# Two stacked model blocks: a reordered projection and delta rule, and compression weights loaded ahead

## The chip, the cores and the metric

One core of a Trainium2 chip runs the whole program. The metric is the device time of one execution, in microseconds (us). The kernel before takes 2895.86 us, the median of three runs (2894.96 to 2896.51).

## The reference

256 tokens of width 1024 in fp32 pass through a first block of two layers and a second block of four. What matters here:

```
first block, for l in 0, 1:
  mod = silu(c) @ ada_w[l] + ada_b[l]          # 1024 x 9216: shifts, scales and gates of the layer
  x += 0.5 (1 + g1) * swiglu(modulate(x))      # width 2816
  h = modulate(x);  qkv, z, b, a, q_lat, kv_lat, k_pe, gates = split(h @ w_in)
  q, k, v = silu(causal_conv4(qkv));  q, k to unit length
  o_a = gated_delta_rule(q, k, v, g, beta)     # 8 heads of 128, chunks of 64 tokens
     per chunk: t_inv = (I + m)^-1,  m strictly lower triangular 64 x 64
  o_b = latent attention;  x += (1 + g2) * (mixed branches @ w_out);  second swiglu
second block, layers 0 and 3 (NSA): block compression of keys and values
     gelu(windows @ w1) @ w2 with w1 of 2048 x 256, then compressed, chosen and window attention
```

## The kernel before

One program per engine is written out by hand, and each engine runs its instructions in that order. All weights come as **units** of at most 1 MB, numbered in one list (`unit`, `cols`, `plan_ffn`, `plan_ada`, lines 195 to 290). SyncE loads unit u into one of four raw buffers once unit u-4 is through with it (`sync_program`, line 2878). For most units ScalarE then writes the rounded high part to one of three `wsp` buffers and VectorE the rest (line 348 `ready_act`, line 363 `ready_dve`); TensorE multiplies both parts. `reach` (line 307) says how far ahead of unit u these splits may be issued: three splits past u. Units of ada_w are not split: VectorE adds them up in eight steps (`ada_step`, line 388), TensorE sums the partitions (`ada_pe`) and VectorE adds the bias (`mod_dve`). Units of how "raw" (the NSA compression weights) are multiplied from the raw buffer itself.

**Projection and convolution** (`conv_pe` line 1239, `conv_act` 1274, `conv_dve` 1317). w_in's first 3072 columns are twelve units of 256 columns, qkv 0 to 11; the unit of 16 columns for b and a ("ba") stands third in the list. Units 0 and 1 are multiplied before the norm's root is known (`lins_early`, 490: chunks of unit 0, the sum of squares, chunks of unit 1, the spread of the root, the rest). Then come ba, whose chunks wait for the normalized input pair by pair, and unit 2. After each unit i from 2 to 9 TensorE sums the squares of unit i-2 in head channels, once ScalarE has them (semaphore `SQQ`):

```
                if 2 <= i < 10:
                    e.wait_ge(*SQQ.at((l, i - 2)))
                    sums(e, bank["qksum", l], 4 * (i - 2), SQ2[i % 2], 2).then_inc(*CSUM.up((l, i - 2)))
```

The squares of unit 0 come by this chain: VectorE scales the product (`scaled`), ScalarE adds the shift and makes the last tap's product, VectorE adds three taps for each of two tiles (`taps_dve`, 1340), ScalarE takes silu and the square (`conv_silu_act`, 1307). `gates_act` and `gates_dve` (1355, 1372) make beta and the decay from ba.

**Delta rule** (`delta_pe` 1477, `delta_act` 1650, `delta_dve` 1686, `delta_pool` 1763). There are four chunks c; a tile has the 64 tokens of a chunk for head 2hp on partitions 0 to 63 and for head 2hp+1 on 64 to 127 (q = 0, 1), four head pairs side by side. GpSimd and VectorE make m and the decayed qk. The inverse T is built in six levels s = 0 to 5 by doubling blocks. At each level, chunk by chunk: 8 products x = m T (64x64 each), VectorE masks x into XX, 8 products add T x to T in PSUM and (s < 5) 8 add its transpose, ScalarE copies T and its transpose (512 columns together) back to UT. Operand and result of a product use the same half of the partitions, so the two heads of a pair use two of the array's four 64x64 tiles. Level 0 starts from an identity that eight matmuls of 512 columns write. Between the levels stand the transposes of k and v (`turned`) and two ada_w parts. The tail (`un`, `w`, `ws`, `kv`, `outs`) runs the recurrence; two more ada_w parts stand in it. `take` and `give` (406, 423) pass the eight PSUM banks on, first given first taken.

**NSA** (`nsa_pe` 2454, `nsa_act` 2550, `nsa_dve` 2597). TensorE multiplies kvc 0 and 1, gate, q 0, the first half of the compression weights (two raw units), q 1, the second half (two raw units), q 2, a transpose after GELU, q 3 and so on.

Of the kernel before, what the change touches and what calls it, by code (L numbers as in the profile page):

```python
# [17 lines left out]
NR = 4  # L18
# [12 lines left out]
NCONST = C_FREQ + 8  # L31
# [78 lines left out]
def build(nc, A, cst, out):  # L110
    ctx = ExitStack()
    with ctx:  # L112
# [51 lines left out]
        out_in = count("out_written")  # L164
        RAW = [count(f"raw{i}_landed") for i in range(NR)]
# [70 lines left out]

        w256 = [256]
        plan_ada(8)
        for l in range(2):
            plan_ffn(2 * l, A["ffn1_w1"][l], A["ffn1_w3"][l], A["ffn1_w2"][l], True)  # L240
            wi = A["w_in"][l]
            cols(("qkv", l), wi, w256 * 2, 0)
            cols(("ba", l), wi, [16], 4096)
            cols(("qkv", l), wi, w256 * 10, 512)
            cols(("z", l), wi, w256 * 3, 3072)
            plan_ada(4, "steps")
# [10 lines left out]
            cols(("up", l), A["mla_w_q_up"][l], [384] * 4, 0, "rope")  # L257
            cols(("up", l), A["mla_w_kv_up"][l], [512] * 4, 0)
# [8 lines left out]
        for i in range(4):  # L267
            kind, j = i % 3, i // 3
            if kind == 0:
# [4 lines left out]
                for s in range(2):  # L274
                    for n in "kv":
                        unit(("cmp", j), A[f"nsa_cmp_{n}_w1_2"][j].rearrange("(k p) n -> p k n", p=128)[:, 8 * s:8 * s + 8, :], 8, 256, "raw")
                    cols(("q", j), wi, w256, 256 + 256 * s)
# [212 lines left out]
        def lins_early(e, us, ps, n):  # L490
# [748 lines left out]
        def conv_pe(e, l, n):  # L1239
            for i in range(12):  # L1240
                if i == 2:
                    take(e, ("qksum", l))
                    u = U["ba", l][0]
                    b = take(e, ("ba", l))
                    lin(e, u, b, hH, hL, h_pairs(n)).then_inc(*MM.up(u))
                    give(("ba", l), GAC.at((l, "rows")))
# [7 lines left out]
                lin(e, u, b, hH, hL).then_inc(*MM.up(u))  # L1254
                give(("qkv", l, i), CVA.at((l, i)))
                if i == 2:
# [6 lines left out]
                if i == 4:  # L1263
                    decays_pe(e, l)
# [9 lines left out]
        def conv_act(e, l):  # L1274
            for i in range(12):
                if i == 2:
                    gates_act(e, l)
                if i == 5:
# [38 lines left out]
        def conv_dve(e, l):  # L1317
# [4 lines left out]
            for i in range(12):  # L1322
                if i == 2:
                    gates_dve(e, l)
                if i == 5:
                    decays_dve(e, l)
                    sums_dve(e, l)
                if i:
# [7 lines left out]
                if i >= 10:  # L1336
                    for q in range(2):
                        unit_dve(e, l, 2 * i - 16 + q)
# [95 lines left out]
        XX = [ar(6144 + 256 * c, 4, 64) for c in range(4)]  # L1434
        UT = [ar(9216 + 512 * c, 2, 4, 64) for c in range(4)]
        KT, KD, VT = ([ar(o + 512 * c, 4, 128) for c in range(4)] for o in (11264, 7168, 15360))
# [22 lines left out]
        def level(s):  # L1459

            return C[:, C_LV + 64 * s:C_LV + 64 * s + 64].unsqueeze(1).broadcast_to([128, 4, 64])
# [5 lines left out]
        def delta_ada(l):  # L1467

            return [nada[U["z", l][2] + 1 + i] for i in range(4)]
# [7 lines left out]
        def delta_pe(e, l):  # L1477
# [17 lines left out]
            for t in range(2):  # L1495
# [7 lines left out]
            def turned(name, c):  # L1503
# [6 lines left out]
                give((l, name, c), DVC.at((l, "kd", c)) if name == "kt" else DAC.at((l, "v", c)))  # L1510

            for s in range(6):
                for c in range(4):
                    b = take(e, (l, "x", s, c))
                    if s:
                        e.wait_ge(*DAC.at((l, "ut", s - 1, c)))
                    else:
                        e.wait_ge(*DVC.at((l, "m", c)))
                    for hp, q in both():
                        u = UT[c][half(q), 0, hp, :] if s else ident[half(q), half(q)]  # L1520
                        ins = e.matmul(P[b][half(q), 64 * hp:64 * hp + 64], MKQ[c][half(q), 0, hp, :], u, start=True, stop=True)
                    ins.then_inc(*DMM.up((l, "x", s, c)))
                    give((l, "x", s, c), DVC.at((l, "x", s, c)))
                if s == 0:
                    for c in range(4):
                        b = take(e, (l, "ut", c))
                        for q in range(2):
                            i64 = ident[half(q), half(q)]
                            e.matmul(v3(P[b][half(q), :], 8), i64, i64.unsqueeze(1).broadcast_to([64, 8, 64]), start=True, stop=False)
                    e.wait_ge(*SIL.at((l, 11)))  # L1530
                if s < 4:
                    turned("kt", s)
                    turned("vt", s)
                if s in (3, 4):
                    ada_pe(e, delta_ada(l)[s - 3])
                for c in range(4):
                    b = bank[l, "ut", c]
                    e.wait_ge(*DVC.at((l, "x", s, c)))
                    for hp, q in both():
                        t = UT[c][half(q), 1, hp, :] if s else ident[half(q), half(q)]  # L1540
                        x = XX[c][half(q), hp, :]
                        ins = e.matmul(P[b][half(q), 64 * hp:64 * hp + 64], t, x, start=False, stop=s == 5)
                    if s < 5:
                        for hp, q in both():
                            t = UT[c][half(q), 1, hp, :] if s else ident[half(q), half(q)]
                            x = XX[c][half(q), hp, :]
                            ins = e.matmul(P[b][half(q), 256 + 64 * hp:320 + 64 * hp], x, t, start=False, stop=s == 4)
                    ins.then_inc(*DMM.up((l, "ut", s, c)))
                    if s == 5:
                        give((l, "ut", c), DAC.at((l, "ut", 5, c)))  # L1550

            def un(c):
                b = take(e, (l, "un", c))
                e.wait_ge(*DAC.at((l, "ut", 5, c)))
# [6 lines left out]
            def w(t):  # L1561
                bs = [take(e, (l, "w", t, q)) for q in range(2)]
                for r in range(2):
                    c = 2 * t + r
                    e.wait_ge(*DAC.at((l, "ut", 5, c)))
# [72 lines left out]
            ada_pe(e, delta_ada(l)[2])  # L1638
# [6 lines left out]
            ada_pe(e, delta_ada(l)[3])  # L1645
# [4 lines left out]
        def delta_act(e, l):  # L1650
# [3 lines left out]
            for c in range(4):  # L1654
                e.wait_ge(*DMM.at((l, "eb", c // 2)))
                e.activation(EB[c].rearrange("p h j -> p (h j)"), P[bank[l, "eb", c]][:, :], ACT.Exp).then_inc(*DAC.up((l, "eb", c)))
            for i in (10, 11):
                conv_silu_act(e, l, i)
            ready_act(e, U["qkv", l][11])
            for s in range(6):  # L1660
                n = 512 if s < 5 else 256
                if s < 4:
                    e.wait_ge(*DMM.at((l, "vt", s)))
                    for hp in range(4):
                        ins = e.activation(VT[s][:, hp, :], P[bank[l, "vt", s]][:, 128 * hp:128 * hp + 128], ACT.Copy, scale=pair_col(BB, s, hp))
                    ins.then_inc(*DAC.up((l, "v", s)))
                for c in range(4):
                    e.wait_ge(*DMM.at((l, "ut", s, c)))
# [1414 lines left out]
```

## Time and profile before

| | us |
|---|---|
| median of three runs | 2895.86 |
| the profiled execution | 2896.91 |
| its span | 2895.1 |
| TensorE matmuls busy | 2795.2 (97%) |
| VectorE busy | 2106.0 (73%) |
| ScalarE busy | 1474.1 (51%) |
| GpSimd busy | 153.7 (5%) |

Times in the rows are microseconds from the span's start. PE is TensorE's matmuls, PEld its weight loads, DVE VectorE, ACT ScalarE, POOL GpSimd, SP SyncE. In brackets stands how long the engine was idle before the first instruction of the row, and who ended it. A matmul of fp32 operands has two records in the trace, one of fp32r operands has one. L65 (matmul), L68 (transpose), L71 (activation), L74 (tensor_tensor), L82 (scalar_tensor_tensor) are helpers that all code calls.

### The profile page before, as it was taken

The page shows a single profiled execution, that of the slowest core. Times are in us where ns is not written, and L with a number is a line of the kernel's source. Part 1 is how long each engine was busy: PE and PEld are TensorE (multiplying, and loading weights), DVE is VectorE, ACT ScalarE, POOL GpSimd, SP SyncE. Part 2 cuts the span into 40 slices and gives each one's busy share as a digit, 9 for nine tenths or more (in the row PEclk, how much of TensorE's full clock was granted, in tenths as well). Part 3 has the DMA queues.
Part 4 walks back from the last instruction along what each step waited for, and adds up shares of the span by engine and source line. Part 5 has one row for each costly group of instructions (what it writes and reads, how often), then busy time and mean ns, then how long its engine had stood idle before and what let it go on. Part 6 is the DMA issues. An engine that isn't in the chain of part 4 may idle for free. (4 is left out here: it accounts for less than half of the span.)

```text
span 2895.1 us, 53856 instructions
## 1 busy us (share of the span) xinstructions
PE 2795.2 (97%) x22820; PEld 2500.7 (86%) x22820; DVE 2106.0 (73%) x3321; ACT 1474.1 (51%) x2010; POOL 153.7 (5%) x257
## 2 busy tenths in 40 slices
PE   7998999999999989999999999999999999999998
PEld 6888899888888888998988878889788988887887
DVE  7886867669888877676786587765776677667774
ACT  3546644555455466445554355544554355435552
POOL 1000000200000000002000040000100000005000
PEclk9999999999999999999999999999999999999999
DMA  9775336537767743374475624555365556561552
GB/s 304 252 247 162 105 117 214 180 131 257 247 216 259 258 146 118 103 224 156 150 250 182 207 90 132 186 178 175 117 204 181 184 174 196 170 220 59 170 186 96
DMA packets 516703, 521.42 MB, mean 180 GB/s; under 512 B 16503, under 2 KB 513728, under 8 KB 516464
## 3 DMA queue, kind: packets, MB, share of 16 engines
q1 hardware_dynamic: 513856, 517.28, 54.9%
q8 instruction: 180, 2.95, 0.4%
q0 software_dynamic: 816, 0.27, 0.1%
q10 hardware_dynamic: 1792, 0.44, 0.1%
q14 instruction: 59, 0.48, 0.1%
HBM read 516.90 MB, written 1.05 MB: 179 GB/s over the span
## 5 line engine op out<-in xcount | busy, mean ns | idle before, releaser
L65 PE MATMUL P<-HX,wsp 128*128 128x512 f32 (+1 forms) x9920 | 1536.5, 317 | 28.0 <-DVE wsp L74 21.8
L65 PEld LDWEIGHTS P<-HX,wsp 128*128 128x128 f32 x9920 | 1386.7, 190 | 157.9 <-issue 28.8
L74 DVE TENSOR_TENSOR wsp<-raw,wsp 128x2048 fp32r<-128x2048 f32 (+3 forms) x440 | 945.8, 2152 | 321.1 <-ACT wsp L71 320.3
L71 ACT ACTIVATE wsp<-raw 128x2048 fp32r<-128x2048 f32 (+3 forms) x440 | 790.7, 1799 | 521.0 <-PE P L65 445.2
L65 PE MATMUL P<-FG,wsp 128*128 128x256 f32 (+1 forms) x2816 | 496.5, 338 | 0.0
L65 PEld LDWEIGHTS P<-FG,wsp 128*128 128x128 f32 x2816 | 428.7, 188 | 62.8 <-DVE wsp L74 1.2
L71 ACT ACTIVATE arena<-P 128x512 f32<-128x512 f32 (+3 forms) x379 | 210.6, 564 | 484.6 <-PE P L65 470.1
L74 DVE TENSOR_TENSOR arena<-arena,P 128x512 f32<-128x512 f32 (+2 forms) x226 | 147.0, 652 | 164.6 <-ACT arena L71 134.9
L82 DVE SCALAR_TENSOR_TENSOR ACC<-raw,sm,ACC 128x256 f32<-128x256 f32 x476 | 230.9, 485 | 16.6
L65 PE MATMUL P<-arena 64*64 64x64 f32 (+9 forms) x4000 | 226.8, 260 | 14.9 <-ACT arena L71 9.6
L65 PEld LDWEIGHTS P<-arena 64*64 64x64 f32 (+3 forms) x4000 | 182.6, 146 | 55.6 <-issue 31.0
L65 PE MATMUL P<-GX,wsp 128*128 128x256 f32 (+1 forms) x1592 | 227.8, 303 | 0.8 <-DVE GX L74 0.8
L65 PEld LDWEIGHTS P<-GX,wsp 128*128 128x128 f32 x1592 | 210.3, 191 | 13.5 <-DVE GX L74 1.1
L79 POOL TENSOR_SCALAR arena<-arena,sm 128x128 f32<-128x128 f32 x192 | 104.9, 557 | 1268.5 <-DVE sm L97 1265.9
L71 ACT ACTIVATE arena<-arena,sm 128x128 f32<-128x128 f32 (+1 forms) x206 | 91.5, 449 | 56.1 <-DVE sm L88 51.8
L71 ACT ACTIVATE arena<-arena 128x512 f32<-128x512 f32 (+2 forms) x174 | 105.3, 613 | 20.3 <-DVE arena L74 17.3
L71 ACT ACTIVATE FG<-arena 128x512 fp32r<-128x512 f32 x88 | 55.6, 632 | 114.0 <-DVE arena L74 102.4
L74 DVE TENSOR_TENSOR arena<-arena 128x512 f32<-128x512 f32 x144 | 98.8, 690 | 7.7 <-ACT arena L71 3.3
L68 PE MATMUL P<-C,arena 128*128 128x128 f32 x410 | 67.8, 298 | 30.3 <-POOL arena L79 15.6
L71 ACT ACT_TABLE_LOAD x62 | 79.5, 1283 | 17.1 <-issue 10.3
L88 DVE CUSTOM_DVE_ANT_0 arena<-P,C 128x128 f32<-128x128 f32 x192 | 59.7, 351 | 35.7 <-PE P L65 35.3
L68 PEld LDWEIGHTS P<-C,arena 128*128 128x128 f32 x410 | 48.4, 150 | 42.9 <-DMA arena<-in_norm_ffn 11.0
(119 smaller groups left out, 1556.1 us busy)
## 6 DMA issues: line engine op xcount, KB each, us to landing
raw<-in_ffn_w SPq DMA_DIRECT2D x120, 1024.0 KB, 5.1
raw<-in_ada_w SPq DMA_DIRECT2D x72, 1024.0 KB, 5.0
raw<-in_w_in SPq DMA_DIRECT2D x52, 1024.0 KB, 5.0
raw<-in_ffn_w_gate SPq DMA_DIRECT2D x44, 1024.0 KB, 5.1
raw<-in_ffn_w_up SPq DMA_DIRECT2D x44, 1024.0 KB, 5.1
raw<-in_ffn_w_down SPq DMA_DIRECT2D x32, 1024.0 KB, 5.0
raw<-in_nsa_w_in SPq DMA_DIRECT2D x20, 1024.0 KB, 8.0
raw<-in_ffn_w SPq DMA_DIRECT2D x16, 768.0 KB, 4.4
```

The costliest lines, as they stand in the source:

```text
L65: return self if self.e is None else self.e.matmul(*a, skip_group_check=True, **k)
L68: return self if self.e is None else self.e.transpose(*a)
L71: return self if self.e is None else self.e.activation(*a, **k)
L74: return self if self.e is None else self.e.tensor_tensor(*a)
L79: return self.e.tensor_scalar(o, a, s1, None, op0) if op1 is None else self.e.tensor_scalar(o, a, s1, s2, op0, op1)
L82: return self if self.e is None else self.e.scalar_tensor_tensor(out=o, in0=a, scalar=s, in1=b, op0=op0, op1=op1)
L88: return self.e.tensor_tensor_reduce(o, a, b, scale, 3.0e38, ALU.add, ALU.min, least)
```

## The change

- The ba unit moves from behind qkv unit 1 to behind unit 2, in the list and on all engines; unit 2 now takes the input pair by pair. `decays` moves one unit later. In `conv_act` the splits of units 0 and 1 are issued ahead of the shift. `lins_early` does five more chunks' worth of matmuls (30 in place of 18) between the sum of squares and the spread. VectorE scales the last two k tiles ahead of the taps of unit 10.
- The delta rule works on two halves t of two chunks. Level 0 needs no product: VectorE makes (masked m) + I. Then five levels: 16 products per half whose result goes to the other half of the partitions, one mask of 512 columns, and an update in which T's and the transpose's products alternate over all four 64x64 tiles. T and its transpose lie in two banks and are copied one after the other.
- Two ada_w parts per layer leave the delta levels for the latent up-projections (behind up 1 and up 4).
- The first half of the NSA compression weights (2 MB per NSA layer) is loaded in a feed-forward before it (f = 3 and 6) into free room; GELU is issued ahead of ScalarE's next splits, and VectorE makes the keys ahead of one split.
- In the first feed-forward the ada_w parts stand one unit pair earlier.

```diff
-                if ada and i % 4 and i < 11:
+                if ada and (i % 4 and i < 11 if f else i % 4 != 3 and i < 10):
...
-            cols(("qkv", l), wi, w256 * 2, 0)
+            cols(("qkv", l), wi, w256 * 3, 0)
             cols(("ba", l), wi, [16], 4096)
-            cols(("qkv", l), wi, w256 * 10, 512)
+            cols(("qkv", l), wi, w256 * 9, 768)
             cols(("z", l), wi, w256 * 3, 3072)
-            plan_ada(4, "steps")
+            plan_ada(2, "steps")
...
+            for i in range(4):
+                cols(("up", l), A["mla_w_q_up"][l], [384], 384 * i, "rope")
+                if i == 1:
+                    plan_ada(1)
+            for i in range(4):
+                cols(("up", l), A["mla_w_kv_up"][l], [512], 512 * i)
+                if i == 0:
+                    plan_ada(1)
...
             chunks_of(0, range(5))
             sums_pe(e, n)
-            chunks_of(1, range(3))
+            chunks_of(1, range(4))
+            chunks_of(0, (5,))
             spread_pe(e, n)
-            chunks_of(0, (5,))
-            chunks_of(1, range(3, 6))
+            chunks_of(1, range(4, 6))
...
                 if i == 2:
                     take(e, ("qksum", l))
+                if i == 3:
                     u = U["ba", l][0]
                     b = take(e, ("ba", l))
-                    lin(e, u, b, hH, hL, h_pairs(n)).then_inc(*MM.up(u))
+                    lin(e, u, b, hH, hL).then_inc(*MM.up(u))
...
-                lin(e, u, b, hH, hL).then_inc(*MM.up(u))
+                lin(e, u, b, hH, hL, h_pairs(n) if i == 2 else None).then_inc(*MM.up(u))
...
                 if i < 2:
+                    ready_act(e, u)
                     e.wait_ge(*CVS.at((l, i, "scaled")))
...
+                if i == 11:
+                    for q in range(2):
+                        unit_dve(e, l, 6 + q)
                 if i:
                     taps_dve(e, l, i - 1)
...
+            def first(t):
+                u, v = take(e, (l, "u", t)), take(e, (l, "t", t))
+                e.wait_ge(*DVC.at((l, "t1", t)))
+                for x in range(8):
+                    for q in range(2):
+                        i64, w = ident[half(q), half(q)], T1ST[t][half(q), x, :]
+                        o = 256 * (x // 4) + 64 * (x % 4)
+                        e.matmul(P[u][half(q), o:o + 64], w, i64, start=x == 0, stop=False)
+                        ins = e.matmul(P[v][half(1 - q), o:o + 64], i64, w, start=x == 0, stop=False)
...
+            def update(s, t):
...
+                    for q in range(2):
+                        T, W = UT[c][half(1 - q), 1, hp, :], XX[t][half(1 - q), x, :]
+                        ins = e.matmul(P[u][half(q), o:o + 64], T, W, start=False, stop=s == 5)
+                        if s < 5:
+                            ins = e.matmul(P[v][half(1 - q), o:o + 64], W, T, start=False, stop=s == 4)
...
+            first(0)
+            first(1)
+            for s in range(1, 6):
+                products(s, 0)
+                products(s, 1)
+                if s < 3:
+                    eb(s - 1)
+                if s >= 2:
+                    turned("kt", s - 2)
...
+                if s >= 3:
+                    turned("vt", s - 3)
...
+                update(s, 0)
+                update(s, 1)
...
+                for j, f in ((0, 3), (1, 6)):
+                    if u in U["f3", f][4:6]:
+                        i = U["f3", f].index(u) - 4
+                        e.wait_ge(*MM.at(U["f3", f][0]))
+                        e.dma_start(W1[i], cmp_src(j, "kv"[i], 0)).then_inc(*w1_in[i].up(j, 16))
```

## Rows read from the trace of the kernel before

**Rows 1.** The page, part 1: busy time by engine.

```profile
PE 2795.2 (97%) x22820; PEld 2500.7 (86%) x22820; DVE 2106.0 (73%) x3321; ACT 1474.1 (51%) x2010; POOL 153.7 (5%) x257
```

**Rows 2.** Stretches, delta rule of layer 0: length, busy by engine, PEclk, DMA share, GB/s.

```profile
333.50:343.50 10.00, 7.67 (x105) 5.51 (x104) 9.75 (x19) 5.71 (x11) 5.99 (x8) 1.00 0.26 90
343.50:385.90 42.40, 41.23 (x1153) 37.69 (x1155) 29.22 (x62) 21.88 (x44) 0.00 (x0) 1.00 0.24 78
385.90:404.70 18.80, 18.41 (x534) 16.90 (x530) 14.68 (x46) 6.28 (x14) 0.00 (x0) 1.00 0.35 115
```

**Rows 3.** Groups by form, TensorE, 343.5 to 385.8.

```profile
L65 PE MATMUL P<-arena 64*64 64x64 f32 x894 | 27.6, 219 | 1.1 <-issue 1.1
L65 PE MATMUL P<-C,arena 64*64 64x64 f32 x128 | 4.6, 219 | 1.0 <-DVE arena L74 1.0
L68 PE MATMUL P<-C,arena 128*128 128x128 f32 x32 | 4.4, 280 | 0.0
L65 PE MATMUL P<-C 64*64 64x512 f32 x16 | 3.6, 589 | 0.0
L65 PE MATMUL P<-arena,C 64*64 64x64 f32 x64 | 2.6, 220 | 0.0
```

**Rows 4.** Two-tile groups, and a four-tile stretch (`w`): timeline, then stretches of TensorE.

```profile
350.53 0.63 PE L65 MATMUL P<-C,arena 64*64 64x64 f32 x16
...
353.33 0.63 PE L65 MATMUL P<-C,arena 64*64 64x64 f32 x16
...
387.75:388.50 0.75, 0.75 (x62) 1.00 0.00 0
```

**Rows 5.** Timeline around the start of the delta rule, layer 0.

```profile
336.89 3.71 PE L65 MATMUL P<-arena 128*64 128x128 f32 x64 [1.36 <-DVE arena L74]
...
340.53 1.99 PE L65 MATMUL P<-arena,C 64*128 64x512 f32 x8
...
349.75 1.29 DVE L74 TENSOR_TENSOR arena<-P,sm 128x512 f32<-128x512 f32 x2 [3.67 <-PE P L68]
...
351.21 0.60 ACT L71 ACTIVATE arena<-P 128x512 f32<-128x512 f32 x1
```

**Rows 6.** Stretches of the projection, layer 0 (columns as in rows 2).

```profile
256.50:261.90 5.40, 0.04 (x1) 0.07 (x1) 2.49 (x3) 5.40 (x9) 0.00 (x0) 0.71 0.01 2
261.90:269.50 7.60, 7.60 (x50) 7.47 (x50) 6.24 (x8) 6.78 (x7) 0.00 (x0) 0.76 0.62 198
```

**Rows 7.** Timeline of the projection, layer 0.

```profile
253.60 2.89 PE L65 MATMUL P<-HX,wsp 128*16 128x256 f32 x24
...
255.88 0.91 ACT L71 ACTIVATE arena<-arena,sm 128x256 f32<-128x256 f32 x2 [1.64 <-DVE arena L74]
...
257.50 1.89 ACT L71 ACTIVATE wsp<-raw 128x2048 fp32r<-128x2048 f32 x1
...
264.62 1.29 ACT L71 ACTIVATE arena<-arena 128x512 f32<-128x512 f32 x2 [0.54 <-DVE arena L82]
...
278.18 0.63 PE L65 MATMUL P<-C,arena 128*64 128x1 f32 x16 [1.96 <-ACT arena L71]
```

**Rows 8.** Timeline of the two NSA layers.

```profile
1635.22 3.67 PE L65 MATMUL P<-raw,arena 128*64 128x256 f32 x32 [0.80 <-DVE arena L74]
...
1653.31 8.14 PE L65 MATMUL P<-HX,wsp 128*128 128x256 f32 x48 [4.88 <-DVE wsp L74]
...
1661.43 6.00 PE L65 MATMUL P<-HX,wsp 128*128 128x256 f32 x48
...
2564.72 3.67 PE L65 MATMUL P<-raw,arena 128*64 128x256 f32 x32 [0.78 <-DVE arena L74]
...
2587.42 6.00 PE L65 MATMUL P<-HX,wsp 128*128 128x256 f32 x48
```

**Rows 9.** Timeline, second feed-forward of layer 0: the norm's root.

```profile
644.96 0.43 PE L68 MATMUL P<-C,sm 128*128 128x128 f32 x2 [0.93 <-DVE sm L97]
```

**Rows 10.** Timeline, seven of the eight steps of an ada_w part on VectorE.

```profile
554.02 3.61 DVE L82 SCALAR_TENSOR_TENSOR ACC<-raw,sm,ACC 128x256 f32<-128x256 f32 x7
```

More of the change, by code:

```diff
@@ L30 @@
 C_FREQ = C_HM + 8
-NCONST = C_FREQ + 8
+C_I64 = C_FREQ + 8
+NCONST = C_I64 + 64
 class Count:
@@ L274, in build @@
                 for s in range(2):
-                    for n in "kv":
-                        unit(("cmp", j), A[f"nsa_cmp_{n}_w1_2"][j].rearrange("(k p) n -> p k n", p=128)[:, 8 * s:8 * s + 8, :], 8, 256, "raw")
+                    if s:
+                        for n in "kv":
+                            unit(("cmp", j), cmp_src(j, n, s), 8, 256, "raw")
                     cols(("q", j), wi, w256, 256 + 256 * s)
@@ L1467, in delta_ada, with delta_steps @@
         def delta_ada(l):
-            return [nada[U["z", l][2] + 1 + i] for i in range(4)]
+            return [nada[U["z", l][2] + 1 + i] for i in range(2)]
+        def delta_steps(l):
+            return [(j, q) for j in delta_ada(l) for q in range(8)]
         def sums_dve(e, l):
@@ L1494, in delta_pe, with eb @@
                 give((l, "qk", c), DVC.at((l, "m", c)), DVC.at((l, "qd", c)))
-            for t in range(2):
+            def eb(t):
                 bs = [take(e, (l, "eb", 2 * t + r)) for r in range(2)]
@@ L1509, in turned @@
                 ins.then_inc(*DMM.up((l, name, c)))
[L1510 to L1529, printed above, removed]
-                    e.wait_ge(*SIL.at((l, 11)))
[L1531 to L1550, printed above, removed]
@@ new lines, in products @@
+            def products(s, t):
+                b = take(e, (l, "x", s, t))
+                e.wait_ge(*DAC.at((l, "u", s - 1, t)))
+                for x in range(8):
+                    c, hp = 2 * t + x // 4, x % 4
+                    for q in range(2):
+                        ins = e.matmul(P[b][half(1 - q), 64 * x:64 * x + 64], MKQ[c][half(q), 0, hp, :], UT[c][half(q), 0, hp, :], start=True, stop=True)
+                ins.then_inc(*DMM.up((l, "x", s, t)))
+                give((l, "x", s, t), DVC.at((l, "x", s, t)))
@@ new lines, in values @@
+            def values(c):
+                e.wait_ge(*DMM.at((l, "vt", c)))
+                for hp in range(4):
+                    ins = e.activation(VT[c][:, hp, :], P[bank[l, "vt", c]][:, 128 * hp:128 * hp + 128], ACT.Copy, scale=pair_col(BB, c, hp))
+                ins.then_inc(*DAC.up((l, "v", c)))
+            for s in range(6):
+                if s in (1, 2):
+                    for c in (2 * s - 2, 2 * s - 1):
+                        e.wait_ge(*DMM.at((l, "eb", s - 1)))
+                        e.activation(EB[c].rearrange("p h j -> p (h j)"), P[bank[l, "eb", c]][:, :], ACT.Exp).then_inc(*DAC.up((l, "eb", c)))
+                if s == 5:
+                    values(2)
+                for a in range(2 if s < 5 else 1):
+                    if s == 2 and a:
+                        conv_silu_act(e, l, 10)
+                        conv_silu_act(e, l, 11)
+                    for t in range(2):
+                        name = "ut"[a]
+                        e.wait_ge(*DMM.at((l, "ut", s, t)))
+                        e.activation(UTP[t][:, :, 256 * a:256 * a + 256], v3(P[bank[l, name, t]][:, :], 2), ACT.Copy).then_inc(*DAC.up((l, name, s, t)))
+                if s >= 3:
+                    values((0, 1, 3)[s - 3])
@@ L1720, in delta_dve @@
                         e.tensor_tensor(qe, qe, eb, ALU.mult).then_inc(*DVC.up((l, "qe", c)))
-                if s == 1:
-                    ready_dve(e, U["qkv", l][11])
-                n = (5, 1, 5, 5, 3, 3)[s]
-                for j, q in steps[first:first + n]:
+                n = (0, 0, 4, 2, 2)[s - 1]
+                for j, q in steps[done:done + n]:
                     ada_step(e, j, q)
-                first += n
-            for j, q in steps[22:24]:
-                ada_step(e, j, q)
+                done += n
+            ready_dve(e, U["qkv", l][11])
             def state(c):
@@ L2428, in build @@
         KCB = ar(16032, 4, 32)
+        W1 = [ar(17920 + 2048 * i, 8, 256) for i in range(2)]
         HG, GTS = ar(16160, 256), ar(16416, 256)
@@ L2634, in nsa_dve @@
             for s in range(2):
-                for i in range(2):
-                    ready_dve(e, U["cmp", j][2 * s + i])
                 queries(1 + s)
```

170 lines of the change are left out of this document (101 added, 69 removed).

## The prediction

> **What bounds the kernel now.** I read the page first: TensorE is busy for 97% of the span, VectorE for 73% [rows 1]. So an edit pays where it takes TensorE work away or closes a stretch in which TensorE stands still. The view of stretches over the delta rule of layer 0 says which of the two it is there: 42.4 us of levels with TensorE busy for 41.2, at full clock, with little DMA [rows 2]. The levels are TensorE's. In the groups by form [rows 3] the 64x64 matmuls are 1086 records, two for each of the code's 544 products; then 4.4 us of transposes and 3.6 us for the identity of level 0. The timeline and a short stretch [rows 4] give the rates. Seven groups of 16 records start evenly within 2.80 us (first and last shown), so a record of the two-tile form takes 2.80/96 = 29.2 ns. In the tail, `w` runs over all four tiles: 62 records touch 0.75 us, and as a record lasts some 0.22 us [rows 3], that is 62 in 0.97 us, 15.6 ns each. The projection has another kind of loss: TensorE stands still for 5.4 us after ba, and the 48 matmuls behind it lie in 7.6 us at a mean granted clock of 0.76 [rows 6] where a unit's otherwise take 6.0 [rows 8]; behind unit 3 it waits 1.96 us more for the squares [rows 7]. NSA has a wait of 4.88 us for a late split of q 2 [rows 8].
>
> **Delta rule, TensorE's work.** Gone: 1088 records at 29.2 ns (31.8 us) and 3.6 us of identity. New: `first` 64 and `update` of levels 1 to 4 256 products, 640 records over four tiles; 160 masked products and 32 of the last update, 384 records over two tiles, 11.2 us. For four tiles the row gives 15.6 ns and half the two-tile rate 14.6; I take 14.6, because the measured stretch has its edges in it: 9.3 us (15.6 would add 0.6). The transposes stay at some 4.1 us, the exponents' matmuls (2.0 us [rows 5]) move in between the levels, and two ada_w sums (0.8 us) move to the up-projections. Loop: 26.6 us of work where there were about 40.3.
>
> **Delta rule, waits.** With two halves there is less to do while a result travels, so I followed the chain with these durations: 0.93 us for 16 products of a half, 0.93 for its 32 updates over four tiles, 0.69 for a 512-column VectorE operation (two in 1.29 [rows 5]), 0.6 for a ScalarE copy [rows 5], 0.1 between engines. A level is at least 3.7 us plus its filler (1.0 to 1.5). Level 2's successor waits for ScalarE, which loads silu's table and does the activations of units 10 and 11 ahead of the transposes' copies (about 0.9 us of wait). At level 5 the transpose of v needs a bank that only ScalarE's scaling of v releases (0.5 us). Levels 1 to 5 come to 4.9, 5.4, 5.8, 5.3 and 5.8 us. Ahead of them, the k tiles are scaled before unit 10's taps, so the qk products start without the 1.36 us of idle [rows 5]; then `first` waits twice for VectorE's two extra passes per half (0.45 and 1.2 us). From 333.5 to the end of the levels I get 36.6 us against 52.4: 10.0 + 42.4 [rows 2]. That is **15.8 us a layer, 31.6 in all**. The tail of 18.8 us is kept: it has two ada_w parts as before. Bounds: without any wait the stage would take 32.3 us (20 saved); if the halves never overlapped, a level would be 2 x 3.4 plus filler, about 8 us, and 3 us would be saved.
>
> **Small unit behind unit 2.** The wait of 5.4 us for unit 2's split goes. What is late next is in the quoted lines of `conv_pe`: behind unit 2 stands the wait for the squares of unit 0, which so far unit 2's own lateness hid. That chain starts at 255.88 and ends at 264.62 + 1.29 = 265.9 [rows 7]. In the new order it starts 1.5 us later, since twelve more matmuls (6.0/48 = 0.125 us each) stand ahead of the root's spread; it has one split of 1.89 us less in it on ScalarE, and not the 0.54 us for the taps. It ends at about 265.0. Unit 2, not held up, ends at 253.5 + 6.0 = 259.5. So TensorE waits 5.5 us there, with ba, bat, gates and unit 3 queued behind. After it come 0.6 of sums, 2.9 of ba and the clock's loss: unit 3 starts near 270, as before (261.9 + 7.6 and the sums' 0.6). The later wait of 1.96 us is followed by the same chain one unit later, about 1.8. Net: **+0.2 a layer**; between -7 (both hidden) and +2.
>
> **NSA.** From the first compression products to q 3 TensorE takes 1661.43 - 1635.22 + 0.80 = 27.0 us in layer 0 and 23.5 in layer 3 [rows 8]. The work in it is 2 x 3.6 + 2 x 6.0 + 0.3 = 19.5. With the first half loaded ahead, q 2's load no longer waits for a raw buffer that compression weights hold, the keys are a 2.3 us split earlier, and GELU is ahead of a split that waits for a DMA. All waits go: 7.5 + 4.0 = **11.5 us**. kv 0 is loaded once the second half is through and would be split some 1.5 us before it is needed; if it is late, up to 3 us come back. The 2 MB each, loaded in the feed-forwards, lie under four raw buffers of lead there; if that cover were gone, each would hold up one split by the time of a load, once per layer.
>
> **The rest.** The later spread helps where VectorE's split holds up the root (0.93 us of idle [rows 9]), but everything behind the spread then comes 0.4 to 1.0 us later on a VectorE that later holds up TensorE: +0.6 for each of three feed-forwards, **+1.8**. ada_w at the up-projections: a part is 4 us of VectorE (seven steps in 3.61 [rows 10]), which had 29.2 of 42.4 us to do in the levels [rows 2] and waits for ScalarE in every up-projection; its sums on TensorE merely move. If that cover is gone, up to 4 us a part return, and that is in the range. Earlier ada_w in the first feed-forward, GpSimd's new order, the constants, the third unit's longer split ahead of the root: nothing, since VectorE and the queues have room there.
>
> **Sum:** -31.6 + 0.4 - 11.5 + 1.8 = -40.9 us. The profiled execution took 2896.9, which gives 2856.0; it lay 1.0 above the median, so against the median **2855**. Own range 2847 to 2865.
>
> **Rivals.**
> *The small unit does close the gap.* If the squares of unit 0 come by 259.5, each layer gains 5.4 and the clock's 1.6 more: 14 us, 2841. For it: ScalarE has idle time ahead of the shift. Against: the chain above, whose links are all serial. 0.12.
> *Latency takes the place of work.* The levels wait for every copy: 2 us more each, 10 a layer, 2875. For it: ScalarE has 2.4 us of copies a level plus v's scaling, near the level's length. 0.10.
> *Row halves of the array that share a bank take turns.* In `w` each bank is written from one half of the rows; `first` and `update` write each bank from both. Then 640 records take 29.2 ns: 9.3 us a layer more, part of it in waits that exist anyway, so 7.5: 2870. Against: the two-tile groups already write one bank from both halves, and their tile spends 58.4 ns on a record, against 62.4 in `w`. 0.07. The Trainium skill (TensorEngine Tiling (Array Packing), "Gotcha 1: PSUM Pressure") says that different row tiles cannot access the same PSUM bank simultaneously; by that rule this rival would be the outcome. The two-tile rows speak against it where the halves write different partitions.
> *The clock.* The other side: the short waits of the levels bring TensorE to 1.2 GHz for most of the stage. At half clock its 51 us of matmuls there (32.3 ahead of the tail, 18.4 in it) cost up to as much again, some 45 beside the waits: 15.8 saved become 29 lost a layer, 2895.9 + 58 - 11.5 + 2.2 = 2945. It decides from about 20 us a layer of work at 1.2 GHz on. For it: a 5.4 us wait does bring the clock down [rows 6]. Against: 10 us with TensorE busy for 7.7 kept 1.00 [rows 2]. 0.05.
>
> **Numbers.** The forecast has 0.66. The range 2839 to 2877 holds it, the first three rivals and the bounds of the levels. A difference under 0.2% (5.8 us) could hardly be told from no change here. Faster by more: 0.94; within: 0.02 (a part of the clock's case); slower: 0.04.
>
> **What would show it.** In the profile after: levels of 5 to 6 us and the stage from the first decay matmul to `un` near 37 us; four-tile records near 15 ns apart; a TensorE wait of about 5 us behind unit 2 and ahead of ba, ended by ScalarE; none ahead of q 2, with the loads of w1 within the feed-forwards; PEclk 1.00 over the levels. Wrong it would be if update groups ran at 29 ns, if the levels took 8 us, or if ba followed unit 2 at once.

## The result, and the profile after

| | median of the runs, us | ratio to before, with 95% interval |
|---|---|---|
| before | 2896.19 (2894.96 to 2902.33, four runs) | |
| after | 2869.61 (2867.01 to 2872.98, four runs) | 0.9905 (0.9886 to 0.9923) |

The change is worth 26.6 us, 0.95%; the forecast was 41 us. 2869.6 lies above the forecast's own range (2847 to 2865) and inside the wider one (2839 to 2877), which takes in three of the rivals. The profiled execution took 2871.2 us (span 2869.4), against 2896.9 (span 2895.1). The page, part 1, against [rows 1]:

```profile
PE 2768.4 (96%) x22660; PEld 2473.0 (86%) x22660; DVE 2103.5 (73%) x3299; ACT 1470.6 (51%) x2006; POOL 155.3 (5%) x257
```

TensorE is busy for 26.8 us less and idle for 101.0 us where it was 99.9. Where the time went is seen best by setting the starts of the same matmuls of both timelines side by side: between two of them lies one stage, and the differences add up (but for rounding). The delta rule's row goes from its first decay matmul to the first matmul of `w_branch_a`, so that the z units behind it are in; the next row goes on to the second feed-forward.

| stage | after minus before, us | forecast |
|---|---|---|
| start and first feed-forward | -1.2 | 0 |
| projection, layers 0 and 1 | -0.2, +0.4 | +0.2 each |
| delta rule, layers 0 and 1 | -9.8, -6.0 | -15.8 each |
| latent up-projections, layers 0 and 1 | -0.6, -0.6 | 0 |
| three later feed-forwards | +1.8, +0.9, +1.9 | +0.6 each |
| NSA, layers 0 and 3 | -7.9, -4.4 | -7.5, -4.0 |
| the rest | +0.1 | |
| sum | -25.7 | -40.9 |

So one term failed: the delta rule, by 15.8 us of 31.6. The stretches of it up to the z units, after (first decay matmul to the first product of level 1; to `un`; to the z projection; then the same for layer 1):

```profile
332.04:343.74 11.70, 8.41 (x226) 7.49 (x226) 11.02 (x20) 6.30 (x9) 6.81 (x8) 0.94 0.23 78
343.74:373.61 29.87, 27.64 (x943) 24.40 (x939) 19.79 (x35) 18.65 (x39) 0.00 (x0) 0.96 0.02 4
373.61:393.51 19.90, 18.43 (x539) 16.91 (x533) 14.52 (x42) 7.18 (x17) 0.00 (x0) 1.00 0.51 162
1110.40:1122.19 11.79, 8.50 (x226) 7.58 (x226) 11.02 (x20) 6.29 (x9) 6.88 (x8) 0.94 0.23 79
1122.19:1154.26 32.07, 27.95 (x944) 24.39 (x940) 19.64 (x35) 18.65 (x39) 0.00 (x0) 0.97 0.02 4
1154.26:1173.94 19.68, 18.68 (x536) 16.98 (x532) 14.63 (x42) 7.18 (x17) 0.00 (x0) 1.00 0.51 163
```

Forecast were 9.4 (what 36.6 leaves), 27.2 (the five levels together) and 18.8. Where the kernel before took 52.4 and 18.8 [rows 2], and 52.1 and 19.0 in layer 1, the first two now take 41.6 and 43.9, and the tail 1.1 and 0.7 more. In all three TensorE waits: the timeline of layer 0 says for what.

```profile
339.21 0.24 PE L66 MATMUL P<-C,arena 64*64 64x64 f32 x1 [1.50 <-DVE arena L75]
...
340.15 0.22 PE L66 MATMUL P<-C,arena 64*64 64x64 f32 x1
...
342.16 0.24 PE L66 MATMUL P<-C,arena 64*64 64x64 f32 x1 [1.79 <-DVE arena L75]
...
343.74 3.00 PE L66 MATMUL P<-arena 64*64 64x64 f32 x64
...
347.73 3.96 PE L66 MATMUL P<-arena 64*64 64x64 f32 x192
...
359.12 2.44 PE L66 MATMUL P<-arena 64*64 64x64 f32 x131
362.97 2.02 PE L66 MATMUL P<-arena 64*64 64x64 f32 x61 [1.40 <-issue]
...
385.59 3.47 PE L66 MATMUL P<-arena 128*64 128x64 f32 x76 [1.20 <-issue]
```

Three things: two waits for VectorE ahead of `first`, 1.50 and 1.79 us (forecast 0.45 and 1.2); 64 two-tile records in 3.00 us instead of 1.87, because the granted clock fell to its lower level, 1.2 GHz, behind those waits (0.51 from 342.4 to 343.7 and 0.63 over these 64); and stalls named issue, in which TensorE waits for nothing that the profile shows. VectorE, and then GpSimd, in the same place:

```profile
337.04 2.02 DVE L75 TENSOR_TENSOR arena<-arena,C 128x512 f32<-128x512 f32 x2
338.99 0.74 DVE L75 TENSOR_TENSOR arena<-P,arena 128x256 f32<-128x256 f32 x2
339.76 2.25 DVE L75 TENSOR_TENSOR arena<-arena,C 128x512 f32<-128x512 f32 x2
...
337.35 4.12 POOL L75 TENSOR_TENSOR arena<-arena,C 128x256 f32<-128x256 f32 x4
```

The mask and the identity take 0.9 to 1.1 us a pass, where 0.69 was forecast. The waits of TensorE over the whole program by releaser (total, times, longest), the row of issue:

```profile
PE P L66 <- issue: 7.0, 6, 2.1
```

Before, this was 1.8 us in four waits. The projection, after (compare [rows 6] and [rows 7]):

```profile
252.33 5.90 PE L66 MATMUL P<-HX,wsp 128*128 128x256 f32 x48
263.82 1.02 PE L66 MATMUL P<-C,arena 128*64 128x1 f32 x16 [5.59 <-ACT arena L72]
264.77 11.40 PE L66 MATMUL P<-HX,wsp 128*16 128x256 f32 x72
...
284.71 0.63 PE L66 MATMUL P<-C,arena 128*64 128x1 f32 x16 [1.81 <-ACT arena L72]
```

The wait of 5.59 us that was forecast as 5.5 stands behind unit 2, for the squares of unit 0, with ba and unit 3 queued behind it; the later one is 1.81 us (forecast 1.8). NSA, layer 0 (compare [rows 8]):

```profile
1620.85 3.67 PE L66 MATMUL P<-arena 128*64 128x256 f32 x32
1624.46 6.01 PE L66 MATMUL P<-HX,wsp 128*128 128x256 f32 x48
1630.39 3.67 PE L66 MATMUL P<-raw,arena 128*64 128x256 f32 x32
1634.00 6.02 PE L66 MATMUL P<-HX,wsp 128*128 128x256 f32 x48
1639.86 0.38 PE L69 MATMUL P<-C,arena 128*128 128x128 f32 x2
1640.00 6.00 PE L66 MATMUL P<-HX,wsp 128*128 128x256 f32 x48
```

No wait is left: 19.15 us to q 3, forecast 19.5. And the second feed-forward, where 0.6 us were forecast to be lost and 1.8 were (before, [rows 9], the waits were 0.93 and 0.89):

```profile
638.01 5.80 PE L66 MATMUL P<-HX,wsp 128*128 128x512 f32 x32
644.38 5.82 PE L66 MATMUL P<-HX,wsp 128*128 128x512 f32 x32 [0.56 <-DVE wsp L75]
650.12 0.40 PE L66 MATMUL P<-C,ACC 128*64 128x1 f32 x8
652.07 12.26 PE L66 MATMUL P<-HX,wsp 128*128 128x512 f32 x60 [1.55 <-DVE wsp L75]
```

### The profile page after: what moved, and what is told of

It reads as the page before. It is cut to its first block and busy times, and to the rows that moved or that the text cites. A ratio compares the mean times of both kernels' runs of the same rounds, so it can differ in the third digit from the quotient of the medians.

```text
span 2869.4 us, 53517 instructions
## 1 busy us (share of the span) xinstructions
PE 2768.4 (96%) x22660; PEld 2473.0 (86%) x22660; DVE 2103.5 (73%) x3299; ACT 1470.6 (51%) x2006; POOL 155.3 (5%) x257
## 3 DMA queue, kind: packets, MB, share of 16 engines
q8 instruction: 179, 2.93, 0.4%
## 5 line engine op out<-in xcount | busy, mean ns | idle before, releaser
L66 PE MATMUL P<-arena 64*64 64x64 f32 (+9 forms) x4064 | 218.2, 262 | 17.4 <-ACT arena L72 9.6
L66 PEld LDWEIGHTS P<-arena 64*64 64x64 f32 (+3 forms) x4064 | 172.2, 146 | 61.0 <-issue 36.4
```

Source lines behind the costliest of these rows:

```text
L66: return self if self.e is None else self.e.matmul(*a, skip_group_check=True, **k)
```

## The experiments

Each kernel was timed beside the kernel before on its own chip, so ratios are compared; the changed kernel's is 0.9905. An interval is some 0.0015 to each side, 4 us, so a few microseconds are read from stages of the traces, and only larger differences from the ratios.

**Do the parts add up?** Two kernels start from the one before. `delta_only` takes the hunks of the delta rule, the earlier scaling of k and the two ada_w parts at the up-projections:

```diff
-            plan_ada(4, "steps")
+            plan_ada(2, "steps")
...
+            first(0)
+            first(1)
```

> The kernel before, with the four-tile delta rule, its earlier scaling of k and the two ada_w parts at the up-projections, and nothing else of the change. Theory A: the parts add up, and the traces' -9.8 and -6.0 us of the two delta stages and -0.6 us at each up-projection are the delta rule's own: about 17 us less than before, 2879. Rival: the delta rule is worth what was forecast, near 31 us, and lost the rest to the shifted projection and its clock in the changed kernel; then about 2865.

Measured: 2882.79 us, ratio 0.9948 (0.9936 to 0.9961), 15 us less. By its trace the delta rule's rows of the table are -6.5 and -7.2 us. `nsa_only` takes the NSA hunks:

```diff
+                for j, f in ((0, 3), (1, 6)):
+                    if u in U["f3", f][4:6]:
...
+                        e.dma_start(W1[i], cmp_src(j, "kv"[i], 0)).then_inc(*w1_in[i].up(j, 16))
```

> The kernel before, with the NSA part alone: the first half of the compression weights loaded ahead, GELU ahead of ScalarE's splits, the keys ahead of one split. Theory A: the traces' -7.9 and -4.4 us of the two NSA layers belong to it alone: 12.3 us less than before, and with the clock's chance windows 2883 to 2887 against 2896. Rival: part of that comes from the four raw buffers standing differently after the changed feed-forwards and ada_w order; then 5 to 9 us less.

Measured: 2886.77 us, ratio 0.9956 (0.9942 to 0.9970), 12.8 us less, and -7.9 and -4.4 in its own trace, as in the changed kernel. Theory A held twice. The two ratios together leave 0.9904, the changed kernel's 0.9905: projection and feed-forwards together are worth nothing that these intervals can tell (+3.6 us by the table, the start included). So the delta rule fell short by itself, in an otherwise unchanged kernel.

**VectorE and GpSimd at the start of the delta rule.** `pool_late`:

```diff
+            e.wait_ge(*DVC.at((l, "t1", 1)))
             for c in range(4):
                 e.tensor_tensor(MKQ[c][:, 1], MKQ[c][:, 1], LE...
```

> The changed kernel, with GpSimd's four multiplications for the decayed qk held back until VectorE has made the second half's start of the inverse. In the changed kernel VectorE's two passes per half take 2.02 and 2.25 us, where its 512-column passes on PSUM take 0.69 each, and GpSimd is busy on the same chunks all the while (334.7 to 341.5). Theory A: the two engines slow each other down. Then the passes take near 1.38 us per half, the waits ahead of the two starts fall from 1.50 and 1.79 to about 0.9 and 0.9, and GpSimd's four, alone, take well under 4.1 us; VectorE then waits for them, which may cost some of it again. Rival: two SBUF operands of this form cost 1.0 us whoever else works; the passes stay at 2.0 and 2.2 us.

Measured: 2870.71 us in one run, no gain that one run could tell. In the stage itself there is one. Five traces have the changed delta rule exactly as it is (the changed kernel, `delta_only`, and `spread_back`, `sums_late` and `conv_best` below): from the first decay matmul to the z projection they take 61.1 to 63.2 us in layer 0 and 62.4 to 63.5 in layer 1. Here it is 60.4 in both. The timeline of VectorE, then GpSimd:

```profile
338.70 1.62 DVE L75 TENSOR_TENSOR arena<-arena,C 128x512 f32<-128x512 f32 x2
340.24 0.75 DVE L75 TENSOR_TENSOR arena<-P,arena 128x256 f32<-128x256 f32 x2
341.02 1.42 DVE L75 TENSOR_TENSOR arena<-arena,C 128x512 f32<-128x512 f32 x2
...
342.52 2.80 POOL L75 TENSOR_TENSOR arena<-arena,C 128x256 f32<-128x256 f32 x4 [3.47 <-DVE arena L75]
```

Theory A. With GpSimd out of the way the second half's two passes take 1.42 us instead of 2.25, and GpSimd's own four 2.80 instead of 4.12; the first half's 1.62 still overlap its earlier work. Without GpSimd a pass takes 0.69 us, just what the prediction had. TensorE's two waits are 1.10 and 0.95. The Trainium skill (SBUF — State Buffer, "SBUF: two separate sides") says that VectorE with two SBUF operands and GpSimd take turns on one port pair, whole instructions at a time. That each slows the other agrees with it; that a turn lasts a whole instruction no run here shows.

`start_fast` adds to this that VectorE does half of unit 10's taps later:

```diff
-                    taps_dve(e, l, i - 1)
+                    taps_dve(e, l, i - 1, (0, 1) if i < 11 else (0,))
...
+            taps_dve(e, l, 10, (1,))
             for c in range(4):
```

> The changed kernel; VectorE does the second half of unit 10's taps (1.5 us) behind the start of the inverse instead of ahead of the masks, and GpSimd's four multiplications for the decayed qk are held back as well. Theory A: TensorE's waits ahead of the two starts of the inverse are VectorE's order of work: the first falls from 1.50 to about 0.3 and the second from 1.79 to about 0.9, and with less idle time the clock stays at 1.00 in level 1: 2 to 4 us a layer, 2862 to 2866. Rival: the taps then stand ahead of the release of the banks for level 1's products, and the wait only moves: 2869 to 2871.

Measured: 2868.11 us, ratio 0.9899 (0.9882 to 0.9915): less than expected. The timeline of TensorE:

```profile
338.31 0.24 PE L66 MATMUL P<-C,arena 64*64 64x64 f32 x1 [0.69 <-DVE arena L75]
...
340.43 0.24 PE L66 MATMUL P<-C,arena 64*64 64x64 f32 x1 [0.96 <-DVE arena L75]
...
342.80 0.39 PE L66 MATMUL P<-arena 64*64 64x64 f32 x6 [1.21 <-DVE arena L75]
```

Both theories hold in part: the two waits fell from 3.29 us to 1.65, but a new one of 1.21 stands ahead of level 1, for banks that VectorE frees behind the taps. `eb_first` filled the first wait with work instead:

```diff
+            eb(0)
             first(0)
             first(1)
```

> The changed kernel, with the first half of the exponents' matmuls (four records, 1.13 us) moved from level 1 into the idle time ahead of the first product that starts the inverse. Theory A: that idle time (1.50 and 1.79 us a layer) is free, level 1 does not need the filler, and with less idle time the clock stays at 1.00 through the first level: 1.1 to 2.8 us a layer, 2864 to 2867. Rival: the moved work is the cover of level 1's copies and masks, or the second start waits for a bank that VectorE frees only near 342.7: no gain, 2868 to 2871.

Measured: 2871.98 us, ratio 0.9907 (0.9894 to 0.9921). The rival: the waits are 0.44 and 2.47 us, because the second `first` now needs a bank that VectorE frees late. The sum of the two is 2.91 against 3.29, and the lower clock stayed.

**The stalls named issue.** In the record of transfers, each of the stalls of 0.5 us or more in the two delta stages, before and after, ends 1.2 to 1.5 us behind the end of a 16 KB transfer of the instruction queue. All matmul records and their weight loads are 45,320 instructions; the queue moved 2.93 MB, 65 bytes for each, so one transfer brings some 128 records with their loads. `w_times8` measures the supply, by writing each product of `w` eight times over into the same place:

```diff
-                    for hp, q in both():
+                    for hp, q in both() * 8:
```

> The changed kernel, with each product of the tail's w written eight times over into the same place (1792 more four-tile records in both layers together, 896 a layer). It measures at what rate TensorE is supplied with instructions. In the traces a matmul record and its weight load are two instructions, one transfer of the instruction queue brings 16 KB, and each of the stalls that the profile puts down to issue ends 1.2 to 1.5 us after such a transfer has ended. Theory A: a long four-tile stretch uses up instructions faster than they come, so that stalls stand between the transfers: 128 records or so per transfer and its latency, some 2.5 to 3.5 us, near 20 to 27 ns a record over the stretch, and 18 to 24 us more a layer. Rival: the supply keeps up and the stalls are chance; 14.7 ns a record, 13 us more a layer, no stall.

Measured: 2921.85 us in one run, 26 us a layer more than the changed kernel for 896 records a layer. The instruction queue made 193 transfers in place of 179 for 3584 more instructions of TensorE: 256 for each. The timeline of TensorE, and a stretch of it:

```profile
400.32 2.10 PE L66 MATMUL P<-arena 64*64 64x64 f32 x128 [0.83 <-issue]
403.77 2.09 PE L66 MATMUL P<-arena 64*64 64x64 f32 x128 [1.36 <-issue]
407.50 2.58 PE L66 MATMUL P<-arena 64*64 64x64 f32 x128 [1.63 <-issue]
410.95 0.79 PE L66 MATMUL P<-arena 128*64 128x64 f32 x16 [0.87 <-issue]
```

Theory A, even a little above its figures. TensorE does exactly 128 records, in the first two rows (2.10 - 0.22)/127 = 14.8 ns each, and stands still until 1.2 to 1.5 us behind the end of the next transfer: 128 in 3.45 to 3.73 us from start to start, 27 to 29 ns a record. That is the two-tile rate of 29.2 ns. Four tiles are faster only for as long as instructions are there already. Earlier in the same stage, behind a weight load at some 350 GB/s, one stall was 4.65 us long; whether the load delayed the transfer was not tried. The Trainium skill (Runtime: NRT & Kernel Launch, "Instruction fetch mechanics") says that instructions come in blocks of 256 and that crossing a boundary is mostly hidden; the first agrees with these rows, the second does not hold for dense small matmuls.

What do the four tiles bring in the levels, then? `two_tile` runs each update in two-tile order:

```diff
-                for x in range(8):
...
+                for a in range(2 if s < 5 else 1):
+                    for x in range(8):
```

> The changed kernel, with the update of each level in two-tile order: first the products of T over two tiles, then those of the transpose over the other two; the same instructions, data and waits. It asks what the four tiles themselves are worth, where a long stretch of them is held to one instruction transfer of 128 records in about 3.5 us (27 ns a record). Theory A: in the levels the bursts are short enough to run from what is there already, so four tiles save their 1.87 us in each of four levels, of which the issue stalls of 1.4 to 4 us a layer take some back: this kernel is slower by 4 to 7 us a layer, 2878 to 2884, and the issue stalls of the levels vanish. Rival: instructions and the copies of ScalarE set the pace of the levels anyway; then the order costs less than 1.5 us a layer, 2870 to 2873.

Measured: 2875.61 us, ratio 0.9920 (0.9906 to 0.9933): 0.0015 or 4.3 us above the changed kernel, 2.2 a layer, between the two theories, with intervals that overlap. In the table's rows it is 5.7 and -0.2 us, and 4.2 and 1.3 when the stretches of lower clock in the z units (1.5 us each, one here in layer 0, one in the changed kernel in layer 1) are taken out. What the order does shows in the group of 192 records, an update and the next products:

```profile
347.54 5.28 PE L66 MATMUL P<-arena 64*64 64x64 f32 x192
```

The changed kernel takes 3.96 us for it. The four-tile order saves 1.3 us a level, then, and not the 1.87 of the rates: in this two-tile order a record takes some 26.5 ns, (5.28 - 0.22)/191, and not 29.2. In four levels that is 5.3 us a layer, and the stalls take part of it back. Of TensorE's waits from level 1 to the end of the tail in layer 1, the row of issue (total, times, longest):

```profile
PE P L66 <- issue: 1.5, 3, 0.7
```

The changed kernel has 4.4 us there, and 2.6 in layer 0, where `two_tile` has 1.9. That 2.6 is the lowest of the five traces named above, which have 2.6 to 4.7 us in layer 0 and 3.8 to 4.6 in layer 1. On average their stages are 3.6 and 2.0 us shorter than the 65.7 and 64.8 of `two_tile`, whose second had no stretch of lower clock and theirs had. So four tiles bring some 2 to 4 us a layer net.

**The projection and the feed-forwards.** `spread_back` does the early matmuls in the old order:

```diff
-            chunks_of(1, range(4))
-            chunks_of(0, (5,))
+            chunks_of(1, range(3))
             spread_pe(e, n)
```

> The changed kernel, with only the order of the early matmuls as before: 18 matmuls instead of 30 between the sum of squares and the spread of the norm's root. Theory A: the later spread is what the three later feed-forwards lost (1.84, 0.87 and 1.86 us by the traces), and it starts the chain to the squares of unit 0 some 1.5 us later, so TensorE's wait of 5.6 us behind unit 2 shrinks to about 4.1 in each layer. That is 4.6 + 3.0 us less: about 2862. Rival: the feed-forwards lost their time for another reason, and the wait is set by ScalarE's splits and not by the root; then nothing changes but the wait of 0.9 us ahead of the spread that comes back in some places: 2870 to 2873.

Measured: 2867.54 us, ratio 0.9887 (0.9874 to 0.9901). By stages theory A is right about the feed-forwards: 1.9, 0.9 and 1.9 us come back, all that was lost. In the projection the wait falls from 5.59 to 4.16 us as expected, but a wait of 0.35 ahead of the spread is new and in layer 0 a later stretch at 1.2 GHz takes part of the rest: 0.4 and 1.3 us saved. The expected 2862 was not reached: in its trace stretches of lower clock stood elsewhere, and the row behind the delta rule of layer 0 alone is 4.1 us longer than in the changed kernel, with only 0.8 us of it a wait. `sums_late` moves the sums of unit 0 behind unit 3:

```diff
+                if i == 3:
+                    sums_of_unit(0)
...
-                if 2 <= i < 10:
+                if 3 <= i < 10:
```

> The changed kernel, with the sums of unit 0's squares moved from behind unit 2 to behind unit 3, so that ba and unit 3 no longer queue behind that wait. Theory A: the 5.6 us are a wait for these squares alone. ba then follows unit 2 at once and ends near 261.1; unit 3 waits for its split, which VectorE ends near 263.0, and it ends near 269 instead of 276.1: 7 us a layer, about 2856, and the granted clock stays at 1.00 behind unit 2. Rival: VectorE and ScalarE are the bound of this stretch anyway; the wait comes back in front of unit 3 or behind it, and at most 2 us a layer are saved, 2866.

Measured: 2866.74 us, ratio 0.9889 (0.9874 to 0.9904), 3.0 and 2.0 us less in the two projections.

```profile
253.76 8.62 PE L66 MATMUL P<-HX,wsp 128*128 128x256 f32 x72
264.53 7.47 PE L66 MATMUL P<-HX,wsp 128*128 128x256 f32 x48 [2.15 <-DVE wsp L75]
...
281.66 0.63 PE L66 MATMUL P<-C,arena 128*64 128x1 f32 x16 [2.37 <-ACT arena L72]
```

Half of each theory. The wait was for the squares alone: ba follows unit 2 at once and 5.6 us are won up to the end of unit 3. But 2.4 us stand one unit later, for the squares of unit 2 on a ScalarE that loads three tables there. So `conv_best` has the old early order, the sums of units 0 and 1 behind unit 3, and those of 2 and 3 behind unit 5:

```diff
+                if i == 5:
+                    sums_of_unit(2)
+                if 3 <= i < 10 and i != 4:
+                    sums_of_unit(i - 2)
```

> The changed kernel, with the early matmuls as before (18 ahead of the spread), the sums of units 0 and 1 behind unit 3 and those of units 2 and 3 behind unit 5; nothing is changed in the delta rule. It splits the 19.4 us by which the combination beat the changed kernel. Theory A: 4.6 us are the feed-forwards, and the projection gives 6 and 8 us in the two layers, as the trace of the combination shows: 18 us less than the changed kernel less what the delta rule gave (4): 2853 to 2856. Rival: the projection's gain there came with the delta rule's new start, through the clock; then no better than 2860.

Measured: 2853.99 us, ratio 0.9844 (0.9831 to 0.9857): 0.0061 or 17.7 us below the changed kernel, theory A. `best2` adds VectorE's and GpSimd's order of `start_fast` (its edits are the three shown).

> All that seems to help put together: the early matmuls as before (18 ahead of the spread), the sums of units 0 and 1 behind unit 3, those of units 2 and 3 behind unit 5, and VectorE's and GpSimd's new order at the start of the delta rule. Theory A: the parts add up: 4.6 us from the feed-forwards, 3 and 3.9 us a layer from the projection (the second for the later wait of 2.4 us and the clock behind it), 2 to 4 us a layer from the start of the delta rule: some 22 us, 2848. Rival: ScalarE, with its table loads and splits, bounds the projection, and the waits come back one unit later: 2858.

Measured: **2850.19 us** (2849.78 to 2851.63), ratio 0.9838 (0.9823 to 0.9853), which beats both kernels; theory A but for 2 us. Its projection, layer 0:

```profile
252.60 8.62 PE L66 MATMUL P<-HX,wsp 128*128 128x256 f32 x72
261.94 5.99 PE L66 MATMUL P<-HX,wsp 128*128 128x256 f32 x48 [0.71 <-DVE wsp L75]
...
283.26 1.02 PE L66 MATMUL P<-C,arena 128*64 128x1 f32 x16 [0.94 <-ACT arena L72]
```

What was 5.59 and 1.81 us of waiting is 0.71 and 0.94. The start of the delta rule adds 0.0006 to `conv_best`, less than can be told from ratios; in the traces its stage up to the z projection is 2.1 us shorter in each layer (60.4 and 60.9 against 62.5 and 63.0).

## Why the prediction was right and wrong

**Right: which way, and where the time is not.** The small unit's term came out part by part: a wait of 5.5 us (5.59) behind unit 2, ended by ScalarE, unit 3 near 270 (270.1), 1.8 us later (1.81), and -0.2 and +0.4 us net for a forecast +0.2. Rival A, that the gap closes, fell: it closes only when the sums move too, as `conv_best` does. NSA gave 12.3 us for 11.5, alone and together. The ada_w parts cost nothing at the up-projections (-0.6 each).

**Wrong: the delta rule, 15.8 us a layer.** Its work was right and its waits were not.
- The term "0.69 for a 512-column VectorE operation", for the two extra passes a half: alone they take just that, but beside a working GpSimd 0.9 to 1.1 us. What the two engines do to each other was put at nothing. The waits for `first` are 1.6 us longer a layer than followed; `pool_late` took 1.2 of it away, and the other 0.4 was not traced.
- "PEclk 1.00 over the levels": the rival on the clock had the mechanism and not the size. The lower clock over the second `first` and level 1's products cost 0.65 and about 1 us. That it was not the 29 us of that rival is right: the clock was 0.96 and 0.97 over the levels. That the waits brought it is read from the order of the rows: with the same waits of 1.50 and 1.79 us it came in eight of the ten stages of the five traces, and with the 2.05 us of `pool_late` in neither of two.
- "Loop: 26.6 us of work", as if TensorE were given instructions at any rate. This was missing altogether: 2.6 us of issue stalls in layer 0 and 4.4 in layer 1 (1.1 and 0.6 before; some 4 in both layers by the five traces). The row of short w groups from which the four-tile rate came could not show it; 1.1 us of issue in [rows 3] were the hint.

For layer 0 this is 1.6 + 0.65 + 1.1 + 1.4 in the levels + 1.2 in the tail = 6.0 of the 6.0 us that are missing; for layer 1 1.6 + 0.65 + 1.0 + 3.8 in the levels + 0.6 in the tail + 1.5 behind it = 9.1 of 9.8. The remaining 0.7 was not traced. The 1.5 is no doing of the delta rule. It lies in the second z unit:

```profile
1181.70:1186.00 4.30, 4.30 (x30) 0.60 0.05 9
```

(TensorE's busy time, then the granted clock.) In the 17 us ahead of it TensorE waited once, for 0.62 us; the same matmuls had 1.00 in layer 0; and in `nsa_only`, whose delta rule is the old one, the same 1.5 us are lost at this place. Up to the z units the delta rule saved 9.8 and 7.5 us. Levels 1 to 5 would be 4.9 to 5.8 us long; from update to update it is 5.5, 5.9, 6.8 and 5.8 in layer 0. Rival B (10 us a layer more, through waits for copies) comes near in sum, for the wrong reason: the waits ended by ScalarE are 0.7 and 0.3 us in a layer.

**Rival C, that row halves which share a bank take turns, fell.** The 64 records of the first `first` run over four tiles with both row halves in one bank; they start from 339.21 to 340.15 at 2.4 GHz, 14.9 ns each. The Trainium skill (TensorEngine Tiling (Array Packing), "Gotcha 1: PSUM Pressure") rules this out, and the rows do not bear it out where the halves write different partitions. Its price of 7.5 us a layer, some 6 of it for the updates, was too high as well: in `two_tile` they take 5.3 us more, and 2 to 4 us net.

**Wrong in size: the later spread.** (The list of the change says five chunks more; by its diff it is two, 12 matmuls: 30 in place of 18.) "+0.6 for each of three feed-forwards" was 1.8, 0.9 and 1.9, and `spread_back` gives them back. 0.3 to 0.9 us are longer waits; the rest, 1.5 where it occurs, is the clock behind a wait of 1.55 us where there had been two of 0.9. The term counted waits and left out what the clock adds to them.

## What to carry to other kernels

When a stage's work is halved, ask whether what feeds TensorE can follow: other engines, and the instructions themselves, 128 small fp32 records and their loads to a transfer here. When a wait is left standing in front of other work, move what waits: that, with the old order of the early matmuls, was worth 18 us without a new instruction. Price a wait with the lower clock it may bring, and take an elementwise pass's time from a row in which the other engines do what they will do beside it.

## What the runs showed of the hardware

- Long four-tile stretches of 64x64 fp32 matmuls run at 27 to 29 ns a record, held by the instruction transfers; bursts run at 14.8. This was not expected. In the delta rule it shows as some 4 us of stalls a layer, which take back part of the 5.3 us that four tiles bring in the updates.
- Two SBUF passes of VectorE took 2.25 us beside GpSimd and 1.42 alone; GpSimd's four took 4.12 and 2.80.
- The same instructions had the lower clock behind a wait of 1.5 us in one execution and not in another. In the third feed-forward (the changed kernel, then `eb_first`):

```profile
849.25 11.40 PE L66 MATMUL P<-HX,wsp 128*128 128x512 f32 x64 [1.54 <-DVE wsp L75]
```

```profile
849.38 12.98 PE L66 MATMUL P<-HX,wsp 128*128 128x512 f32 x64 [1.55 <-DVE wsp L75]
```

Over the first 6.8 us of these groups the granted clock was 1.00 and 0.75. This is 1.6 us, and with some ten such places in a program it makes a single profiled execution uncertain by several microseconds: a stage's difference of 1.5 us in one trace may be no more than that.
